# An encoder layer on one core: the first norm's scale and shift applied to its turned rows, a projection of rounded parts, weight loads in another order, a variance on ACT

## The reference

```python
def layer_norm(x, g, b):
    mu = jnp.mean(xf, -1, keepdims=True)
    var = jnp.mean(jnp.square(xf - mu), -1, keepdims=True)
    return (xf - mu) * lax.rsqrt(var + LN_EPS) * g + b

h = layer_norm(x, ln_in_g, ln_in_b)
# mixer: one input projection of h, three branches (gated DeltaNet, pooling, mLSTM)
y = jnp.einsum('bsrm,rmd->bsrd', branches, w_branch)
gate = jax.nn.sigmoid(gate_pre.reshape(nb, ns, N_BRANCH, D_MODEL))
merged = jnp.sum(gate * y, axis=2)
mix = merged @ w_out
h = layer_norm(alpha * h + mix, ln_mix_g, ln_mix_b)
# router: 2 of 32 experts for each token; expert: silu(x @ w1) * (x @ w3) @ w2
ffn = moe_ffn(h, router_w, router_b, moe_w1, moe_w3, moe_w2)
return layer_norm(alpha * h + ffn, ln_ffn_g, ln_ffn_b)
```

## Time and profile before

| what | value |
|---|---|
| median of 3 runs | 1399.8 us (1399.43 to 1407.07) |
| profiled execution | 1400.41 us, its span 1398.4 us |
| busy: PE, DVE, ACT, POOL | 88%, 57%, 42%, 15% of the span |
| PE's granted clock, mean | 0.956 of full speed |
| front, to the last chunk | 0 to 258 us |
| mLSTM and DeltaNet | 258 to 690.7 us |
| last branch and out projection | 690.7 to 785.3 us |
| router and first gather | 785.3 to 813.9 us |
| 32 experts | 813.9 to 1355.7 us |
| last scatter, final norm, stores | 1355.7 to 1398.4 us |

### The profile page before, as it was taken

One profiled execution on the slowest core, in us unless ns is written; L12 is line 12 of the kernel. 1 busy time (PEld: TensorE's weight loads), 2 busy tenths in 40 slices (PEclk: granted clock), 3 DMA queues, 4 the chain that ended last, 5 costly groups with the idle time before them and its releaser, 6 DMA issues.

```text
span 1398.4 us, 14398 instructions
## 1 busy us (share of the span) xinstructions
PE 1236.5 (88%) x5466; PEld 847.3 (61%) x5466; DVE 800.6 (57%) x963; ACT 583.3 (42%) x728; POOL 212.2 (15%) x190
## 2 busy tenths in 40 slices
PE   2999899877999999898899679999999999999970
PEld 1777778555777778776545445555666665555630
DVE  5675671277444543535523657766666666666627
ACT  3343344453331423212200255556666666556630
POOL 3232061002221312220000011111111111111000
PEclk9999999998999999999999889999999999999995
DMA  7212210101211221202391399999999999999704
GB/s 259 91 61 90 91 60 31 46 1 53 74 56 38 76 61 54 76 23 68 106 404 77 126 347 344 362 397 407 401 402 404 398 388 395 401 397 399 314 11 180
DMA packets 95723, 278.54 MB, mean 199 GB/s; under 512 B 8480, under 2 KB 58272, under 8 KB 70432
## 3 DMA queue, kind: packets, MB, share of 16 engines
q1 hardware_dynamic: 90528, 269.15, 51.5%
q0 software_dynamic: 5120, 8.40, 1.8%
HBM read 267.03 MB, written 18.87 MB: 204 GB/s over the span
## 4 chain that ended last, share of the span: by engine, by line
PE 44%; DVE 3%; DMA 1%; issue 1%; ACT 1%; POOLq 0%; SPq 0%; DVEq 0%; ACTq 0%
PE yb L1773 16%; PE hb L1745 9%; PE hb L1746 8%; PE hb L1969 3%; PE tx L1729 2%; PE hb L1955 2%; PE gb L1760 1%; PE gb L1753 1%; PE yb L1969 1%; DMA xg<-h_dram,rows_all 1%; PE tx L1989 1%; PE yb L1955 0%; DVE stats L2270 0%; DVE h L2277 0%; DVE h L2268 0%
## 5 line engine op out<-in xcount | busy, mean ns | idle before, releaser
L1860 DVE TENSOR_TENSOR wlo<-wraw,whi 128x2048 fp32r<-128x2048 f32 x127 | 285.4, 2287 | 29.0 <-ACT whi L1805 28.9
L1805 ACT ACTIVATE whi<-wraw 128x2048 fp32r<-128x2048 f32 x128 | 241.0, 1908 | 35.0 <-PE hb L1746 35.0
L1773 PE MATMUL yb<-wraw,act_t 128*64 128x512 f32 x512 | 227.9, 598 | 5.9 <-issue 5.9
L1745 PE MATMUL hb<-whi,xs 128*128 128x512 f32 x512 | 211.1, 412 | 1.7 <-DVE xs L1864 1.5
L1746 PE MATMUL hb<-wlo,xs 128*128 128x512 f32 x512 | 201.8, 394 | 0.0
L382 PE MATMUL pj<-h_part,wsplit 128*128 128x512 f32 x672 | 166.1, 407 | 6.3 <-issue 3.7
L1170 PE MATMUL gate_ps<-h_part,gws 128*128 128x512 f32 x576 | 161.2, 420 | 3.3 <-ACT h L1320 3.1
L382 PEld LDWEIGHTS pj<-h_part,wsplit 128*128 128x128 f32 x672 | 129.5, 194 | 38.9 <-issue 10.8
L1773 PEld LDWEIGHTS yb<-wraw,act_t 128*64 128x64 f32 x512 | 67.9, 137 | 140.4 <-issue 138.6
L1170 PEld LDWEIGHTS gate_ps<-h_part,gws 128*128 128x128 f32 x576 | 105.6, 193 | 32.4 <-issue 12.7
L1745 PEld LDWEIGHTS hb<-whi,xs 128*128 128x128 f32 x512 | 97.2, 190 | 45.2 <-issue 26.5
(11 more groups left out here) (365 smaller groups left out, 1626.6 us busy)
## 6 DMA issues: line engine op xcount, KB each, us to landing
wraw<-in_moe_w SPq DMA_DIRECT2D x192, 1024.0 KB, 9.0
h<-in_w_in SPq DMA_DIRECT2D x14, 1024.0 KB, 5.5
h<-in_w_in SPq DMA_DIRECT2D x24, 512.0 KB, 4.5
h_dram<-h SPq DMA_DIRECT2D x8, 512.0 KB, 2.6
h<-in_w_branch SPq DMA_DIRECT2D x16, 256.0 KB, 2.8
kept_dram<-h SPq DMA_DIRECT2D x16, 256.0 KB, 2.1
wraw<-in_w_out SPq DMA_DIRECT2D x2, 2048.0 KB, 14.1
yr<-y_dram SPq DMA_DIRECT2D x4, 1024.0 KB, 7.9
```

The costliest lines, as they stand in the source:

```text
L1745: pe.matmul(bank[:, :], lhs, whi[:, u % NSPLIT, cols], start=(half == 0 and kk == 0), stop=False)
L1773: last = pe.matmul(yb[c][0:SLOTS, :], act_t[:, k, :], raw[:, room, cols], start=(k == 0), stop=(k == FT - 1))
L1805: act.activation(whi[:, u % NSPLIT, :], raw[:, room, :], ACT.Copy).then_inc(S.hi_done.sem, 1)
L1860: dve.tensor_tensor(wlo[:, u % NSPLIT, :], raw[:, room, :], whi[:, u % NSPLIT, :].bitcast(F32), ALU.subtract).then_inc(S.lo_done.sem, 1)
```

## The change

Five edits.

1. **Front, norm.** ACT now writes the rows only centred and scaled; PE turns those. g and b are loaded a second time as columns (gcol, bcol), and are applied in the turned rows: ACT writes h_part[0] with four activations of 128 by 128 for each half tile (L472) in place of one copy, DVE forms the full value from PSUM with four tensor_scalar of 128 by 128 (L650) and subtracts the high part (L653). h itself gets g and b afterwards on POOL, four times a multiply and an add (L752, L753), behind all eight of DVE's turned halves and ahead of POOL's first low part.
2. **Front, order.** The halves are turned in the order half 0 of all tiles, then half 1; PE starts chunk 0's first output tile with half of the channel groups when four halves are there. Chunks 2 and 3 get rooms in yT, so h is stored before chunk 4 only. ACT loads the root's table before the first statistic.
3. **Back, projection.** The merged rows and w_out are split into high parts by ACT and low parts by DVE beside the last branches; the out projection is three fp32r matmuls for each one of before. w_out's first half is loaded ahead of the gated rows of c = 2 and on.
4. **Weights and store.** Only rooms 0 and 1 are filled before the projection; 2, 3, 8, 9 after its seventh half tile, 4 to 7, 10 and 11 after its eighth. The last tile of h is stored from ACT's queue. POOL clears its gather buffers after the projection and not before it.
5. **Tail.** The mean comes from the accumulated sum of the second gated sum (L2337), the variance from a Square on ACT (L2107) with an accumulated sum; bn_stats goes. DVE starts the next tile's first gated sum between. SP reads the overflow flag before it waits for the last scatter, not behind it.

```diff
@@ front
-        raw_rooms += [h[:, 2 * i:2 * i + 2, :] ... for i in range(2)]
+        raw_rooms += [yT[:, i, :, :] ... for i in (1, 0)]
+        raw_rooms += [h[:, 2 * i:2 * i + 2, :] ... for i in range(2)]
...
+                for half in range(2):
+                    pe.wait_ge(turn_low, NT * (half + 1))
+                    for m in range(2):
+                        for k in range(4 * half, 4 * half + 4):
+                            for a, b in PRODUCTS:
+                                last = pe.matmul(pj[m][:, :], w_part[0][a][:, k, m * P:(m + 1) * P], h_part[b][:, k, :],
...
+                    for k in range(4):
+                        kk = 4 * half + k
+                        last = act.activation(h_part[0][:, kk, t * P:(t + 1) * P], gate_banks[n][:, k * P:(k + 1) * P], ACT.Identity,
+                                              scale=gcol[:, kk:kk + 1], bias=bcol[:, kk:kk + 1])
...
+                    for k in range(4):
+                        kk = 4 * half + k
+                        chain.add(dve.tensor_scalar(full[:, k * P:(k + 1) * P], gate_banks[n][:, k * P:(k + 1) * P],
+                                                    gcol[:, kk:kk + 1], bcol[:, kk:kk + 1], ALU.mult, ALU.add))
+                    chain.wait()
+                    dve.tensor_tensor(h_part[1][at], full.rearrange("p (k s) -> p k s", k=4),
+                                      h_part[0][at].bitcast(F32), ALU.subtract).then_inc(turn_low, 1)
...
+                pool.wait_ge(row_in, 32)
+                pool.wait_ge(turn_low, 2 * NT)
                 for t in range(NT):
-                    pool.wait_ge(gmul_ready, t + 1)
-                    pool.wait_ge(ln_in, 32)
+                    chain.link(pool.tensor_tensor(h[:, t, :], h[:, t, :], lng, ALU.mult))
                     pool.tensor_tensor(h[:, t, :], h[:, t, :], lnb, ALU.add).then_inc(h_ready, 1)
@@ back, SP
-                first_weights(sp, range(6))
+                first_weights(sp, range(2))
...
                 for t in range(NT):
                     if t == NT - 1:
+                        sp.wait_ge(out_done, 2 * NT - 1)
+                        first_weights(sp, (2, 3, 8, 9))
                         sp.wait_ge(out_done, 2 * NT)
-                        first_weights(sp, range(6, 8))
-                    sp.wait_ge(h2_ready, t + 1)
-                    sp.dma_start(v["h2_dram"][t * P:(t + 1) * P, :], h2[:, t, :]).then_inc(h2_out, 16)
-                first_weights(sp, range(8, NRAW))
+                        first_weights(sp, (4, 5, 6, 7, 10, 11))
+                    else:
+                        sp.wait_ge(h2_ready, t + 1)
+                        sp.dma_start(v["h2_dram"][t * P:(t + 1) * P, :], h2[:, t, :]).then_inc(h2_out, 16)
...
-                all_scattered(sp, S, NE)
                 with sp.If(left > 0):
+                    all_scattered(sp, S, NE)
                     sync_program(sp, S2, OVER, further, 0)
                     all_scattered(sp, S2, OVER)
+                all_scattered(sp, S, NE)
@@ back, PE
-                        last = pe.matmul(yp[n % 3][:, :], merged[:, k, t * P:(t + 1) * P], wo[:, half, k, :],
-                                         start=(k == 0), stop=(k == KT - 1))
+                        if n == 0:
+                            pe.wait_ge(merged_low, k + 1)
+                        for a, b in PRODUCTS:
+                            last = pe.matmul(yp[n % 3][:, :], merged_part[a][:, k, t * P:(t + 1) * P], wo_part[b][:, half, k, :],
+                                             start=(k == 0 and a + b == 0), stop=(k == KT - 1 and a == 1))
@@ back, ACT
+                def last_rows():
+                    act.wait_ge(h2_ready, NT)
+                    act.dma_start(v["h2_dram"][(NT - 1) * P:NT * P, :], h2[:, NT - 1, :]).then_inc(last_out, 16)
...
-                    act.wait_ge(fstats_ready, t + 1)
-                    act.activation(rstd[:, t:t + 1], mv[:, t, 1:2], ACT.Sqrt, bias=epsc[:, 3:4]).then_inc(fstd_ready, 1)
+                    act.activation(yr[:, t, 1, :], h2[:, t, :], ACT.Square, bias=mv[:, t, 0:1],
+                                   accum_out=mv[:, t, 1:2]).then_inc(fsquared, 1)
```

216 lines of the change are left out of this document (129 added, 87 removed).

## The result

The changed kernel takes **1387.9 us** (median of 4 executions, 1380.57 to 1388.12), the kernel before 1400.1 (median of 4, 1399.43 to 1407.07). The ratio is 0.989, with a 95% interval of 0.985 to 0.993. The prediction was 1383.2 us, in a range of 1373 to 1391. The profiled execution of the changed kernel has a span of 1386.0 us, 12.4 less than the 1398.4 of before, and a mean granted clock of 0.946 (before 0.956).

A forecast was written before the change was run, and what follows sets the result against it. PE was taken as the bound almost everywhere; the terms 0.5 - 11.3 + 0.7 - 6.5 = -16.6 us take the median from 1399.8 to 1383.2 us, in a range of 1373 to 1391.

The forecast's parts named there:

- Front: Start to chunk 7: PE's head start of 11.8 us eaten by POOL's eight instructions and DVE's turns; +0.5, from -3 to +6.
- Projection: Out projection: cheaper fp32r matmuls save 11.0 and an earlier start 1.4, less 1.1 of waits; -11.3, from -12.2 to -9.
- the 1.1 of waits for late splits: Out projection: PE waits 0.5 us at the last group and 0.6 at the second half's weights.
- the rival of a DVE late by 4 us: Out projection: early weights do nothing and DVE's splits come late, giving 1387; 10%.
- Hand over: Projection's end to experts: store lands after 6.5 us, gather starts 1.8 later but issues 1.3 faster; +0.7, from -1.5 to +4.
- the step "0": Expert stage: no edit touches it, so its time was put at 0 change, an expert staying at 16.6 us.
- my own sign: Wrong if the front's end moves by more than 6 us either way, or the expert stage changes its length.
- rival two: Front and hand over cost more: slower halves +4, lower clock after waits, store and gather behind weights +4; 1389 to 1393; 27%.
- Tail: Last scatter to end: early flag read -2.2, tiles of 5.65 us -5.1, small costs at two tiles; -6.5, from -7.2 to -5.
- the likeliest case: Whole kernel: time lands between 1378 and 1388 us; 45%.
- the first rival: Front: the head start survives, chunk 2 starts at 55 to 58, up to 11 us stay; 1372; 15%.

The follow-up runs named there:

- run 1: Changed kernel with POOL's eight multiplies and adds on h moved behind the front's low parts, rooms and stores of h moving too: 1377.96 us, ratio 0.9844.
- run 2: Changed kernel with POOL's four multiplies by g left out and only its four adds kept: 1379.24 us, ratio 0.9848.
- run 3: Kernel before with the changed front alone, nothing of the back: 1400.26 us, ratio 0.9993.
- run 6: The changed kernel measured and traced again, nothing altered: 1385.02 us, ratio 0.9891.
- run 4: Changed kernel with the last store of h on SP's queue, ahead of rooms 6, 7, 10 and 11: 1384.62 us, ratio 0.9881.
- Run 5: Changed kernel with the spare rows' tables and PE's eight small products for them made under the first gather: 1376.96 us, ratio 0.9826.
- run 7: Kernel before with the changed tail alone: 1391.31 us, ratio 0.9932.
- run 8: Changed kernel with the out projection as plain float32 matmuls of the high parts; splits, loads and waits stay: 1398.06 us, ratio 0.9981.

## Why the prediction held, and where it did not

**Front: right, and nearer than its prices deserved.** Runs 1 and 2 show the mechanism, run 3 the sum (0.9993). Chunk 2 was put at 62.7 and started at 62.51, but three prices on the way were off. A half tile takes DVE 2.0 us and not 1.6 (four pieces of 0.34, and 0.69), and ACT 1.44 and not 1.0. DVE began the halves at 18.0 and not 19.0, so PE's start is only 0.75 late (26.25), and the eighth half is 2.2 late (34.04 for 31.8). And POOL's eight took 23.2 us in turns with DVE (34.28 to 57.5), where the working has 25.4 (31.8 to 57.2). The late start and the quicker turns cancel to 0.3, which is luck; I had given 4 us to halves at 2.0.

**Projection: right, by errors that cancel in part.** Products at 0.233 and not 0.229 cost 0.8: the row of 48 in 11.24 has a last product that overlaps by 0.17, and I had taken off more. The start gave 1.9 where I had 1.4. And the 1.1 of waits for late splits did not come in the first trace, PE being busy for 51.26 of 51.30 us; in run 6 PE waits for them twice, 0.5 in all, and the projection is 1.0 longer. So DVE just keeps up, as forecast, and the rival of a DVE late by 4 us is out.

**Hand over: the step that failed first.** The prediction lets the gather start 1.8 us later; it started 4.8 later (795.62 - 773.29 = 22.33, against 802.84 - 785.31 = 17.53). Three parts make up the 3.0. The store took 7.93 and not 6.5 (1.4). It was issued 0.8 later, since PE's 16 logits took 2.74 instead of 1.98: the granted clock falls to 0.50 there in this trace, and stays at 1.00 in the kernel before and in run 6, so this part is not the change's in every execution. And I had set all of the 1.7 between the old store's landing and the old gather against it, when the gather still waits some 1.05 us after a landing (794.57 to 795.62), so that only 0.9 was to be had. Besides, the gather came out 0.7 shorter (7.67 against 8.39) and not 1.3; in run 6 it takes 7.94. The rival had this case at +4, with the right cause. Run 4 puts 2.4 to 2.9 on the store; with the store out, what is left is the logits' 0.7 and a gather that takes 8.86.

**Experts: the step "0" failed.** No edit touches that stage, so I priced it at nothing, and by my own sign I was wrong here: the stage changed its length, by 3.3 us. I had not read its second expert: PE pauses there for 2.75 us before and 2.78 after, and only after does a lower clock come with it. The sentence on rival two, that a pause costs more than itself, was applied to the front alone. Run 5 shows that without the pause there is no fall. Runs 3, 6 and 7 tie the fall to the edits of the projection and the weights, and run 8 shows that it comes without the cheaper products too; by what they act, some 70 us after the projection's end, was not settled, since the granted clock ahead of the pause is 1.00 in both kernels.

**Tail: right, and too small by 1.3.** The flag gave 2.4 (2.43 to 0.06), for 2.2. A tile takes 5.31 and not 5.65: an accumulating operation costs 0.08 on DVE, the small ones 0.17 and 0.09, and neighbouring wide operations overlap, 1.2 on the chain for 1.28 of length, which I had counted at full length. The waits of 0.4 at the first tile and at the last came as worked out: 0.40 beside the table load of 1.28, and 0.32.

**The chances.** The median lies at the upper edge of the likeliest case (1378 to 1388), just under the second rival's: the front as forecast, with the first rival out, the hand over as in the second rival, and the tail better than in either.

## What to carry to other kernels

An edit that frees a bound engine early gains nothing until the next list is shortened too; look at which operations of a third engine were free of cost only because the bound engine had not started, and move them behind what it will need (worth 10 us by the traces here, 7 by the medians). A store that something waits for is best issued ahead of the bulk loads: on a queue with nothing else in it, but with the DMA engines busy for 0.91 of the time, it took 7.9 us for 3.0. And a stage that no edit touches can still lose time at a pause that was harmless before; count each pause of the bound engine in it, and take it away if what fills it can go elsewhere (another 10 us by the traces, 8 by the medians).

## What was not expected of the chip

The same pause had three outcomes. After 2.75, 2.78 and 2.76 us of idle PE before the second expert's third product, its 16 matmuls took 7.05 (kernel before), 9.75 (changed kernel) and 8.75 us (run 8). In the changed kernel the granted clock falls inside the pause (about 841.4, the matmuls start at 842.76), in run 8 only when they have run for about 1.1 us (850.5 for 849.38), and it stays at 0.50 for 7 us and for 3.

Executions of one kernel fall into groups: run 8 has four within 1393.98 to 1394.17 and five within 1398.95 to 1399.88. The profiled one is of the first group, and it is 1.9 us ahead of the changed kernel's trace when the projection starts (718.33 against 720.18), with a front of the same length (chunk 5 at 103.70 and 103.94). The granted clock in the middle differs. Windows of the changed kernel, then of run 8:

```profile
200.00:300.00 100.00, 89.34 (x385) 63.58 (x384) 35.13 (x73) 47.39 (x99) 13.55 (x13) 0.95 0.12 33
```
```profile
200.00:300.00 100.00, 88.59 (x403) 64.28 (x401) 37.47 (x79) 50.25 (x110) 12.98 (x11) 0.98 0.11 31
```

That stretch has the same instructions in both. The changed kernel's own 1380.57 beside three of 1387.8 to 1388.1 may be of that kind; no profile of it was taken, so this stays open. A median of four can move by such a group, which is why the terms above are read from traces, and why run 4's gain is not claimed from its time. A trace is one execution too: the last half tile of h stands 1.5 us later in run 6 than in the first trace of the same kernel.
